# Layer 0's last seven gate projections made in split form, with two blocks of V ahead of them and their weight remainders on GpSimd

## The reference

```python
xn = _rmsnorm(x, norm1_g[l])
proj = xn @ w_in[l]
cq, ckv, k_rope = proj[..., :o1], proj[..., o1:o2], proj[..., o2:o3]
u = proj[..., o3:o4]
gate_a = jax.nn.sigmoid(proj[..., o4:o5])
gate_b = jax.nn.sigmoid(proj[..., o5:])
attn = _mla(cq, ckv, k_rope, cos, sin, ...)      # latent attention
branch_a = attn @ w_attn_up[l]
y = _s5_bidir(u, ...)                            # state-space scan, both directions
z = jax.nn.gelu(y) @ w_glu[l]
branch_b = z[..., :D_MODEL] * jax.nn.sigmoid(z[..., D_MODEL:])
x = x + (gate_a * branch_a + gate_b * branch_b) @ w_o[l]
x = x + _swiglu(_rmsnorm(x, norm2_g[l]), ...)
```

## Time and profile before

| | us |
|---|---|
| median of 3 runs | 1641.42 (1639.15 to 1644.0) |
| profiled execution, its time | 1644.64 |
| profiled execution, its span | 1642.8 |
| PE busy | 1572.3 (96%) |
| DVE busy | 870.6 (53%) |
| ACT busy | 537.2 (33%) |
| POOL busy | 558.0 (34%) |

### The profile page before, as it was taken

How to read it: one execution, slowest core, us unless ns; L and a number is a source line. 1 busy time by engine, 2 the same in 40 slices (tenths; PEclk the granted TensorE clock), 3 DMA queues, 4 the chain that set the end, 5 groups by cost and what they waited for, 6 DMA issues and landing times.

```text
span 1642.8 us, 20801 instructions
## 1 busy us (share of the span) xinstructions
PE 1572.3 (96%) x8296; PEld 1231.1 (75%) x8296; DVE 870.6 (53%) x1234; ACT 537.2 (33%) x853; POOL 558.0 (34%) x274
## 2 busy tenths in 40 slices
PE   8998998999999989999999899989999999999999
PEld 3544667778878868888888788877888788888887
DVE  6995357758736987773221743477594322012210
ACT  2211115663344222223332322467424322123220
POOL 0000012225443454434442322323344444444442
PEclk9999888999999999999999899989999999999999
DMA  7468420023232244444326462100322223222232
GB/s 248 146 186 322 170 95 20 1 77 104 90 118 89 77 141 157 138 156 164 104 90 237 126 231 74 65 1 27 106 100 90 92 88 103 91 102 90 90 103 77
DMA packets 73056, 188.33 MB, mean 115 GB/s; under 512 B 23552, under 2 KB 32000, under 8 KB 68864
## 3 DMA queue, kind: packets, MB, share of 16 engines
q1 hardware_dynamic: 35856, 124.99, 22.4%
q10 hardware_dynamic: 37104, 62.01, 11.4%
HBM read 154.47 MB, written 32.51 MB: 114 GB/s over the span
## 4 chain that ended last, share of the span: by engine, by line
PE 72%; DVE 15%; DVEq 4%; DMA 4%; ACT 3%; issue 1%; ACTq 0%; SPq 0%
PE ps L1467 21%; PE ps L1468 21%; PE ps L1469 21%; PE ps L1604 2%; DMA u_scr<-uT 2%; PE ps L1522 1%; DVE qkTl L1326 1%; PE ps L1581 1%; DVE nmx L1359 1%; DMA U<-u_scr 1%; PE ps L1752 1%; DVE work L912 1%; ACT prob L823 1%; PE ps L1761 1%; DVEq L1039 1%
## 5 line engine op out<-in xcount | busy, mean ns | idle before, releaser
L417 POOL TENSOR_TENSOR wl<-stage,wh 128x1024 fp32r<-128x1024 f32 x204 | 511.4, 2511 | 939.8 <-ACT wh L477 939.7
L477 ACT ACTIVATE wh<-stage 128x1024 fp32r<-128x1024 f32 x204 | 214.0, 1056 | 321.1 <-PE ps L1469 276.0
L1467 PE MATMUL ps<-xg2h,wh 128*128 128x512 f32 x704 | 279.8, 397 | 2.2 <-DVE act L1439 2.2
L1469 PE MATMUL ps<-xg2h,wl 128*128 128x512 f32 x704 | 278.4, 396 | 0.0
L1468 PE MATMUL ps<-xg2l,wh 128*128 128x512 f32 x704 | 278.4, 395 | 0.0
L1522 PE MATMUL ps<-xg,slabs 128*128 128x512 f32 x320 | 150.2, 624 | 16.1 <-DVE gates L1158 10.1
L1467 PEld LDWEIGHTS ps<-xg2h,wh 128*128 128x128 f32 x704 | 132.3, 188 | 35.2 <-issue 3.5
L1468 PEld LDWEIGHTS ps<-xg2l,wh 128*128 128x128 f32 x704 | 132.3, 188 | 32.1 <-issue 0.5
L1469 PEld LDWEIGHTS ps<-xg2h,wl 128*128 128x128 f32 x704 | 132.3, 188 | 31.9
L1467 PE MATMUL ps<-hidh,wh 128*128 128x512 f32 x352 | 140.6, 399 | 2.0 <-DVE hidl L1445 2.0
L1468 PE MATMUL ps<-hidl,wh 128*128 128x512 f32 x352 | 139.9, 397 | 0.0
(11 more groups left out here) (268 smaller groups left out, 2801.5 us busy)
## 6 DMA issues: line engine op xcount, KB each, us to landing
stage<-in_stream SPq DMA_DIRECT2D x204, 512.0 KB, 3.2
CPTR<-ctd_scr ACTq DMA_DIRECT2D x8, 1664.0 KB, 10.0
slabs<-in_stream SPq DMA_DIRECT2D x24, 512.0 KB, 4.7
ctd_scr<-CPp ACTq DMA_DIRECT2D x8, 1152.0 KB, 7.2
in_scr<-BPI ACTq DMA_DIRECT2D x8, 1024.0 KB, 3.9
InT<-in_scr ACTq DMA_DIRECT2D x8, 1024.0 KB, 5.3
toep_scr<-Kf ACTq DMA_DIRECT2D x64, 64.0 KB, 2.7
ctd_scr<-TRa ACTq DMA_DIRECT2D x4, 1024.0 KB, 5.8
```

Of the source, the lines that this page charges most:

```text
L417: pool.tensor_tensor(wl[:, s, :], stage[:, s % STAGES, :], wh[:, s, :].bitcast(F32), ALU.subtract).then_inc(wl_ready, 1)
L477: return act.activation(o, i, ACT.Copy, **kw)
L1467: pe.matmul(o, wt[0], x[0], start=start, stop=False)
L1469: return pe.matmul(o, wt[1], x[0], start=False, stop=stop)
```

## The change

Slabs 17 to 23 of layer 0, which are gates 9 to 15, become split slabs (`RAW = S_GATE + 9`). For that:
- the plain products take X itself, and the gain goes into the weights: each plain slab is multiplied in place (`gain_slab` on ACT, eight 128 x 128 copies or two 128 x 416 ones; slab 0 by DVE), and PE waits for `raw_ready` in place of the load;
- ACT makes `xgh` (eight `normed_x`) and DVE `xgl` (eight more), ACT seven more `split`, POOL seven more remainders;
- `gate(2)` to `gate(6)` move forward in DVE's order;
- on PE, `inputs(0)` comes ahead of gate 9 and `inputs(1)` ahead of gate 10, and the other pieces of the run stand one between two gates;
- on ACT the loads of block 0's and block 1's InT, CPTR and U no longer wait behind taps (`load_taps` is cut out of `load_maps`), and `store_taps(0, 3)` moves behind the loads of block 1;
- tiles move in memory so that this is free of overlaps: the input maps of layer 0 lie in the upper half of `gates`, and gates 8 and 12 therefore wait for their stores (`in_stored`).

```diff
-RAW = S_ATT
+RAW = S_GATE + 9
...
+            def gain_slab(n):
+                act.wait_ge(raw_loaded[n % RAWS], 16 * (n // RAWS + 1))
+                if n == 1:
+                    act.wait_ge(raw_ready, 1)
+                w = LAT if S_LAT <= n < S_GATE else P
+                first, count = (2 * (n - S_LAT), 2) if S_LAT <= n < S_GATE else (0, KT)
+                for i in range(count):
+                    part = raw_slab(n)[:, i * w:(i + 1) * w]
+                    last = copy(part, part, scale=gcol[:, first + i:first + i + 1])
+                last.then_inc(raw_ready, 1)
...
                     turned_map(2)
+                    store_taps(0, 1)
+                    gain_slab(14)
...
+                    turned_map(3)
+                    gain_slab(16)
                     store_turns(0)
-                    turned_map(3)
                     store_taps(0, 2)
                     gate_out(6)
-                    load_block(0, 0)
+                    split(0, S_GATE + 9)
+                    load_maps(0, 0)
+                    load_u(0, 0)
+                    load_taps(0, 0)
+                    split(0, S_GATE + 10)
                     store_cp(0, 3)
                     gate_out(7)
                     taps(0, 3)
-                    store_taps(0, 3)
-                    gate_out(8)
                     for i in range(2):
                         act.wait_ge(in_stored[i], 32)
                     act.wait_ge(cp_stored, 16 * BLOCKS)
+                    load_maps(0, 1)
+                    load_u(0, 1)
+                    split(0, S_GATE + 11)
+                    store_taps(0, 3)
...
                 if l == 0:
-                    dve.wait_ge(col_loaded, 16)
-                    for k in range(KT + 1):
-                        if k < KT:
-                            dve.wait_ge(x_loaded[k], 16)
-                            ts(xg32[:, k, :], X[:, k, :], gcol[:, k:k + 1], None, MUL).then_inc(xl_ready, 1)
...
                     gate(7)
+                    for k in range(KT):
+                        normed_x(0, k)
                     direct_taps(0, 3)
+                    dve.wait_ge(in_stored[0], 32)
                     gate(8)
                     states(0)
                     gate(9)
+                    states(1)
                     gate(10)
                     gate(11)
-                    states(1)
+                    states(2)
+                    dve.wait_ge(in_stored[1], 32)
                     gate(12)
-                    states(2)
                     gate(13)
                     states(3)
                     gate(14)
...
                     taps(0, 3)
-                    gate(9)
                     pe.wait_ge(inT_ready, 2 * BLOCKS)
                     inputs(0)
+                    for k in range(KT):
+                        pe.wait_ge(xl_ready, k + 1)
+                    gate(9)
+                    inputs(1)
                     gate(10)
+                    outputs(0)
                     gate(11)
-                    outputs(0)
-                    inputs(1)
+                    outputs(1)
                     gate(12)
-                    outputs(1)
                     inputs(2)
                     gate(13)
-                    outputs(2)
                     inputs(3)
                     gate(14)
+                    outputs(2)
                     pe.wait_ge(k_ready, BLOCKS)
-                    for c in range(LC):
-                        turned_latents(c)
+                    turned_latents(0)
+                    turned_latents(1)
                     gate(15)
+                    turned_latents(2)
                     outputs(3)
```

More of the change, by code:

```diff
@@ L140, in build @@
         r = Region(0)
-        xg32 = r.take("xg32", [P, KT, SEQ])
-        BPI = [[r.take(f"BPI0{i}", [P, 2, C8, P]) for i in range(2)]]
-        r = Region(0)
+        BPI = [[nc.alloc_sbuf_tensor_at(f"BPI0{i}", [P, 2, C8, P], F32, offset=gates_at + (KT + 4 * i) * SEQ * 4)
+                for i in range(2)]]
         mixh = r.take("mixh", [P, KT, SEQ], F32R)
@@ L191, in build @@
             ra = Region(ffn_top if l else set_at[1])
+            if l == 0:
+                CPp.append(ra.take(f"CPp{l}", [P, CPN]))
+            BB.append(ra.take(f"BB{l}", [P, 2, C32, 2 * GCH]))
+            Call.append(ra.take(f"Call{l}", [P, BLOCKS, 2, C8 * GCH]))
+            Kf.append(ra.take(f"Kf{l}", [P, 2, KW]))
             rot.append(ra.take(f"rot{l}", [P, 3, C32]))
@@ L574, in load_maps, with load_taps @@
                 act.dma_start(CPTR[i][:], ctd_scr[l, b]).then_inc(ctd_loaded[i], 16)
[L575 removed]
+            def load_taps(l, b):
+                i = b % 2
+                act.wait_ge(k_stored, 128 * (BLOCKS * l + b + 1))
                 act.dma_start(Toep[i][:].rearrange("p g o -> p (g o)"),
@@ L649, in _ @@
                     load_maps(l, 0)
+                    load_taps(l, 0)
                     load_maps(l, 1)
+                    load_taps(l, 1)
                 for j in range(4):
-                    if l and j < 3:
+                    if l == 0:
+                        gain_slab(3 + j)
+                    elif j < 3:
                         split(l, S_LAT + 1 + j)
@@ L700, in _ @@
                     taps(0, 1)
+                    gain_slab(13)
                     gate_out(3)
+                    for k in range(0, 4):
+                        normed_x(0, k)
+                    turned_map(2)
                     store_taps(0, 1)
-                    turned_map(2)
+                    gain_slab(14)
                     store_cp(0, 2)
                     taps(0, 2)
+                    gain_slab(15)
                     gate_out(4)
                     gate_out(5)
+                    for k in range(4, KT):
+                        normed_x(0, k)
+                    turned_map(3)
+                    gain_slab(16)
                     store_turns(0)
-                    turned_map(3)
                     store_taps(0, 2)
                     gate_out(6)
-                    load_block(0, 0)
+                    split(0, S_GATE + 9)
[3 more added lines that the diff above has]
+                    split(0, S_GATE + 10)
                     store_cp(0, 3)
@@ L1255, in _ @@
                     output_powers(0, 3, 1)
-                    gate(6)
                     gate(7)
+                    for k in range(KT):
+                        normed_x(0, k)
                     direct_taps(0, 3)
+                    dve.wait_ge(in_stored[0], 32)
                     gate(8)
@@ L1529, in _ @@
                     for k in range(KT):
-                        if j == 0:
+                        if l == 0 and j == 0:
+                            pe.wait_ge(x_loaded[k], 16)
+                        elif j == 0:
                             pe.wait_ge(xl_ready, KT * l + k + 1)
```

91 lines of the change are left out of this document (57 added, 34 removed).

## The result

The changed kernel takes 1632.44 us (median of 7 runs, 1631.11 to 1635.57) against 1641.42 (7 runs, 1639.15 to 1645.43): a ratio of 0.9948 with a 95% interval of 0.9935 to 0.996, or 9.0 us faster. 1626.4 was forecast. The profiled execution took 1631.11, its span is 1629.3.

The account below looks back on a forecast made before the run. PE, busy 96%, bounds the kernel, losing time to waits, a lower clock and plain products in the first 247 us. -15.5 + 0.5 = -15.0 us gives 1629.6 profiled, 1626.4 median; range 1615 to 1638, own range 1622 to 1631 (0.52).

Parts of the forecast that it names:

- Split gates: PE, gates 9 to 15: seven gates of 5.6 us in place of 6.95, 9.5 us off PE.
- DVE's order: VectorE's gates 2 to 6 come sooner; PE's waits of 3.25 and 2.33 us go, 9.1 us won by the last taps.
- First load: Before inputs(0): block 0's U lands at 146 us behind 6.6 us of tap stores; PE idles 11 us.
- the 9.1 us are gone: After gate 9: the wait for the first load eats the 9.1 us won by then, and 2 more.
- the walk: PE's pieces timed one by one to outputs(3), ending at 231.1 us, 15.5 sooner; gate 14 waits 3.9.
- GpSimd: Seven more remainders beside VectorE's operations, mostly hidden by PE's waits: +0.5 us.
- the second load: Before inputs(1): map store lands in 12 us (bounds 10 and 13.5), block 1's U at 160.5; PE waits 4.5 us.
- the second load stays late: Rival: inputs(1) starts at 165 to 169 us, gain only 10.5 to 6.5 us, about 1633; chance 0.17.
- isn't changed: Everything behind outputs(3) starts 15.5 us sooner with its end and keeps its length.
- Scaling weights: ACT scales twelve slabs in eight copies of 0.26 us, about 2 us a slab, hidden by PE's gates: 0 to +0.5.
- the slower rival: ACT can't keep up with scaling at gates 4 to 7: each of five gates 4 us later, 1646.5; chance 0.07.
- the prediction's own signs of being wrong: PE waiting for ACT's slabs, states(2) over 13 us, a copy over 0.4 us, or attention delayed by weights not split in time.

Follow-up runs that it names:

- e2: Changed kernel with gates 9 to 15 of layer 0 plain again, their slabs scaled on ScalarE, order kept: 1641.06 us, ratio 0.9995 to the kernel before.
- e7: Changed kernel with GpSimd writing zeros in place of the remainders of slabs 17 to 23: 1632.52 us, ratio 0.9947 to the kernel before.
- e11: Changed kernel with block 0's loads of maps, U and taps issued ahead of block 2's tap stores: 1630.73 us, ratio 0.9925 to the kernel before.
- e3: Changed kernel with the last output map's store issued ahead of block 0's loads: 1628.61 us, ratio 0.9922 to the kernel before.
- e6: Changed kernel with U loaded ahead of CPTR for blocks 0 and 1 of layer 0: 1628.2 us, ratio 0.9922 to the kernel before.
- e10: Changed kernel with VectorE's gates 2 to 6 put back where the kernel before has them: 1637.62 us, ratio 0.997 to the kernel before.
- e1: Kernel before with only VectorE's gates 2 to 6 issued earlier, measured twice: 1647.11 and 1644.74 us, ratios 1.003 and 1.0018 to the kernel before.
- e12: e4 with block 0's InT and U loaded ahead of block 2's tap stores, the last map's store right behind these, CPTR later: 1622.61 us, ratio 0.9887.
- e4: Changed kernel with gate 9 ahead of the first inputs, gate 10 ahead of the second, later pieces moved to match: 1631.06 us, ratio 0.9934.

## Why the prediction was right in direction and 6 us off in size

**Right.** *Split gates* were to take 9.5 us off PE, gate 9's share hidden: e2 measured 8.6 by the median and 5.7 by the end. *DVE's order*: the waits ahead of gates 6 and 8 for VectorE went. *First load*: "the 9.1 us are gone" was right. That its wait was 11.33 (11 forecast) is luck: the last taps ended 3.3 us later than forecast (138.08 against 134.8), and U landed 3.3 us later (149.3 against 146, past the bound of 147.9). From the second inputs on the walk was followed step for step: 70.6 us forecast from there to the end, 71.7 measured, with a wait of 3.81 ahead of gate 14 where 3.9 stood. *GpSimd*: +0.5 and hidden; by the medians e7 measured nothing.

**Wrong: the second load.** "The last output map's store landed after 13.5 us ... bounds 10 and 13.5, taken 12". It landed after 16.22, outside the bounds, U was issued at 156.44 and not at 151.5, and the second inputs started at 166.08 in place of 160.5. Of these 5.6 us, 4.2 are the store's own time (16.22 for 12), 0.6 its issue (139.22 for 138.6), and the rest U's landing (9.59 for 9) and rounding. They are 5.6 of the 6.6 us by which the end missed the forecast (237.75 against 231.1), and e11 shows that the first load, though late too, adds almost nothing. Its row before showed a moment of landing, not a latency: it was issued at 141.31 and landed 13.5 later, at 154.8; issued 2.1 us sooner now, behind the same loads, it landed at 155.4. The step took the 13.5 as the store's own and let it come sooner with its issue. It also named the 3.4 MB ahead, but not the two slabs that SyncE loads from 141.26 on: the engines moved 5.9 MB from 137 to 155.5 (the stretches above). A sum of bytes would have come nearer. An estimate, made afterwards: 3.4 MB of loads, one or two slabs of 0.5 and its own 1.15 are 5.1 to 5.6 MB, at 350 GB/s 14.5 to 16 us. From the forecast's issue at 138.6 that is 153.1 to 154.6, where 150.6 stood and 155.4 was measured; what is missing isn't shown. e3 bears it out from the other side: with none of these loads ahead the store lands in 6.5 us. The rival "the second load stays late" (165 to 169, about 1633) is what happened.

**Luck.** The prediction says that what follows the end "isn't changed". In the traces it is 4.6 us shorter, and so the profiled execution came out at 1631.11 where 1629.6 was forecast, although the end missed by 6.6. The medians, 9.0 us apart, don't have this help: 1632.44 against 1626.4.

**Mis-sized, and of no account.** *First load*: issuing the tap stores took 9.30 us where 6.6 was taken. They stood behind the same stores of the turns and of the map as before, and took nearly the 9.64 of the earlier trace rows; taking the slab loads away did not empty the queue. In e3 and e6, where they began 2.8 us later, they took 6.10 and were issued by 136.4 all the same (136.8 in the changed kernel). It moved InT's issue to 137.00 (135.4). e11, with the loads ahead of these stores, gained 6.1 us at the first inputs and 0.9 at the end.

**Mis-sized, and nearer to the slower rival than thought.** *Scaling weights* were priced at 0.26 us a copy, and the term at 0 to +0.5; the rows show 0.31 (1.55 for five), and gate 6 waited 2.62 us for its slab and ran 1.9 longer at the lower clock. This wait, one of the prediction's own signs of being wrong, is why the last taps came 3.2 us late (136.92 for 133.7), which the first wait swallowed. e10 shows how close this lies: with the gates a power step later, the same wait is 6.07 us and 5 us of the gain are gone. The prediction saw the crowd on ScalarE, but treated the order of VectorE's gates and the scaling as independent; they aren't.

**Not seen.** That the order alone is slower than before (e1). Its trace shows 10.5 us of waiting for U in place of 1.18 us for U and 3.25 and 2.33 for VectorE; where the 3 to 6 us are lost, no trace shows.

## What to carry to other kernels

When transfers follow each other on full DMA engines, price each by the bytes ahead of it, all queues together, not by the latency that its row showed in another order, and put first what is waited for first: one load moved ahead of a larger one (U ahead of CPTR) won 4.2 us, nearly half of what the whole change did. A step that hides beside a wait is worth nothing until the wait's own cause is moved; find the last load in the chain (here a store that frees its memory), since filling or shortening an earlier wait only moves time into that one. And undo each part of a change alone before crediting it: here the rest of the change was worth 3.7 us without VectorE's order and 9 with it, and that order by itself cost 3 to 6. Last, look behind the point that you aim at: a stage that ends at the lower clock hands a part of its gain back (e12: 3.9 of 11.2 us).

## What the runs showed of the hardware that was not expected

- Issuing eight stores of 64 KB took ScalarE 5.16 to 11.41 us in these kernels (both in e1, at 102.59 and 127.54), 0.65 to 1.4 us each. The longer ones stand right behind 3 MB and more of other transfers (9.64 and 10.40 before, at 127.91 and 145.09). While the last of them drained, from 134 to 137 in the changed kernel, the DMA engines were 78% busy and moved 109 GB/s, where 349 were moved from 137 to 149, with InT and CPTR in the queue.
- A store of 1.15 MB landed in 6.5 us right behind the tap stores (e3), 5.8 with InT and U ahead of these (e12), 12.1 with all four loads ahead of these (e11), and 16.2 right behind four loads (changed).
- One program's stage of 245 us can take 4 us more in one execution than in the next (e1: 244.21, 248.00), 2.4 of it through pieces that run at 1.2 GHz for longer.
- The same instructions behind the stage take 1391.3 to 1391.6 us in seven of these kernels and up to 1396.2 in the others; only for e4 and e12 do the traces show where this begins, a TensorE that comes in at 1.2 GHz.
